# Reordered sums of squares and projection products in the attention heads of a two-layer encoder

## What is computed

```python
h = layer_norm(x, ln_in_g, ln_in_b)
for l in range(DEPTH):
    proj = h @ w_in[l]
    a_q, a_k, a_v, b_u, b_b, b_c, c_u, d_q, d_k, d_v = split_columns(proj)
    out_a = windowed_gqa_sink(...)      # group A: window of 128, sink, 4 query heads
    out_b = short_conv_mixer(...)
    out_c = fourier_mixer(c_u)
    out_d = dense_gqa_blocks(...)       # group D: dense attention, 4 query heads
    mix = jnp.concatenate([rms_norm(o, g[...]) for o in (out_a, out_b, out_c, out_d)], axis=-1)
    h = layer_norm(DN_ALPHA * h + mix @ w_out[l], ln1_g[l], ln1_b[l])
    ffn = jnp.square(jax.nn.relu(h @ w1[l])) @ w2[l]
    h = layer_norm(DN_ALPHA * h + ffn, ln2_g[l], ln2_b[l])
```

## Time and profile before

| | |
|---|---|
| time, median of 3 runs | 1057.16 us (1056.75 to 1057.83) |
| the profiled execution | 1057.18 us, span 1055.1 us |
| TensorE matmuls busy | 1038.5 us, 98% of the span |
| VectorE | 761.5 us, 72% |
| ScalarE | 532.4 us, 50% |
| GpSimd | 116.8 us, 11% |
| granted TensorE clock | 0.998 of full speed |

### The profile page before, as it was taken

One profiled execution on the slowest core, in us unless ns is written; L12 is line 12 of the kernel. 1 busy time (PEld: TensorE's weight loads), 2 busy tenths in 40 slices (PEclk: granted clock), 3 DMA queues, 4 the chain that ended last, 5 costly groups with the idle time before them and its releaser, 6 DMA issues.

```text
span 1055.1 us, 15201 instructions
## 1 busy us (share of the span) xinstructions
PE 1038.5 (98%) x5281; PEld 868.7 (82%) x5281; DVE 761.5 (72%) x1035; ACT 532.4 (50%) x777; POOL 116.8 (11%) x122
## 2 busy tenths in 40 slices
PE   7999999999999999999999999999999999999996
PEld 6888887988888888888888888879888888888885
DVE  7845876878668757758887558677884884785787
ACT  3433666665355255355634247666634643642654
POOL 5200343200000000000002004331000000000003
PEclk9999999999999999999999999999999999999999
DMA  8432023031521521521243410311243134125122
GB/s 292 160 120 80 1 61 121 9 121 59 187 74 40 199 80 40 174 106 53 108 144 139 160 41 22 120 42 49 80 157 122 40 124 156 40 92 186 40 80 80
DMA packets 17378, 105.47 MB, mean 100 GB/s; under 512 B 2016, under 2 KB 2704, under 8 KB 5792
## 3 DMA queue, kind: packets, MB, share of 16 engines
q1 hardware_dynamic: 15984, 98.70, 26.3%
q0 software_dynamic: 1184, 5.86, 1.7%
q10 hardware_dynamic: 144, 0.07, 0.0%
HBM read 101.49 MB, written 2.10 MB: 98 GB/s over the span
## 4 chain that ended last, share of the span: by engine, by line
PE 94%; POOL 2%; issue 1%; ACT 1%; DMA 1%; DVE 0%; DVEq 0%; SPq 0%; POOLq 0%; ACTq 0%
PE bank L465 19%; PE bank L466 18%; PE bank L467 18%; PE bank L815 9%; PE bank L814 9%; PE bank L813 9%; PE bank L753 2%; PE bank L738 2%; PE bank L474 1%; PE bank L644 1%; PE bank L645 1%; POOL w_lo L1816 1%; PE bank L541 1%; POOL x L1911 1%; PE bank L548 1%
## 5 line engine op out<-in xcount | busy, mean ns | idle before, releaser
L465 PE MATMUL bank<-h_hi,w_hi 128*128 128x512 f32 (+1 forms) x688 | 257.8, 375 | 0.0
L466 PE MATMUL bank<-h_lo,w_hi 128*128 128x512 f32 (+1 forms) x688 | 257.5, 374 | 0.0
L467 PE MATMUL bank<-h_hi,w_lo 128*128 128x512 f32 (+1 forms) x688 | 257.5, 374 | 0.0
L813 PE MATMUL bank<-w_hi,hid_hi 128*128 128x512 f32 x448 | 174.4, 389 | 0.0
L815 PE MATMUL bank<-w_hi,hid_lo 128*128 128x512 f32 x448 | 174.3, 389 | 0.0
L814 PE MATMUL bank<-w_lo,hid_hi 128*128 128x512 f32 x448 | 174.3, 389 | 0.0
L1257 DVE TENSOR_TENSOR w_lo<-w_raw,w_hi 128x2048 fp32r<-128x2048 f32 x62 | 141.8, 2287 | 39.2 <-ACT w_hi L929 32.7
L929 ACT CAST w_hi<-w_raw 128x2048 fp32r<-128x2048 f32 x56 | 107.1, 1913 | 85.8 <-PE bank L815 61.5
L466 PEld LDWEIGHTS bank<-h_lo,w_hi 128*128 128x128 f32 x688 | 129.5, 188 | 23.1
L465 PEld LDWEIGHTS bank<-h_hi,w_hi 128*128 128x128 f32 x688 | 129.5, 188 | 23.0
L467 PEld LDWEIGHTS bank<-h_hi,w_lo 128*128 128x128 f32 x688 | 129.5, 188 | 23.1
(11 more groups left out here) (184 smaller groups left out, 1610.3 us busy)
## 6 DMA issues: line engine op xcount, KB each, us to landing
w_raw<-in_weights SPq DMA_DIRECT2D x63, 1024.0 KB, 4.7
w_third<-in_weights SPq DMA_DIRECT2D x23, 1024.0 KB, 4.8
rows<-in_rows POOLq DMA_DIRECT2D x4, 1024.0 KB, 4.7
w_raw<-in_weights SPq DMA_DIRECT2D x4, 512.0 KB, 8.5
out_h<-x SPq DMA_DIRECT2D x8, 256.0 KB, 2.0
x<-in_x SPq DMA_DIRECT2D x3, 512.0 KB, 9.6
dft<-in_dft SPq DMA_DIRECT2D x2, 512.0 KB, 7.0
qk_gain<-in_qk_gain POOLq DMA_DIRECT2D x3, 192.0 KB, 3.5
```

The lines of the kernel that those rows point to most:

```text
L465: pe.matmul(dst, s_hi, m_hi, start=first, stop=False)
L466: pe.matmul(dst, s_hi, m_lo, start=False, stop=False)
L467: return pe.matmul(dst, s_lo, m_hi, start=False, stop=last)
L813: pe.matmul(bank[dst + t][:], s_hi, m_hi, start=start, stop=False, skip_group_check=goes_on)
```

## The change

On TensorE, in `SIDE_STEPS`, the second product of tile 3 of group 2 goes from step 11 to step 12, and the second product of tile 0 of group 3 from step 13 to step 14; DVE's additions (and the statistics and variance of tile 0) move with them. In every even step from 4 to 14 the sum of squares comes behind the transposes of the probabilities. Behind the loop TensorE takes the probabilities of the last pair, then the products of tile 2 (they need quad 6), the sum of quad 6, the values of pairs 14 and 15 in one run, the inverse of quad 7, the second half of tile 0, tile 1, and then the products of tile 3 with the sum of quad 7 between them. On ScalarE the high copy of the second half of tile 0 goes behind the squares of quad 7. On DVE the first low half of tile 0 and the two additions of tile 2 go ahead of the scaling of quad 7, the second low half and tile 1 behind its low part, and its mean behind those. GpSimd's and SP's programs are not changed.

```diff
-    SIDE_STEPS.update({4 * _g + _t: w_items(_g, _t, _t + 1) for _t in range(TOK)})
+    SIDE_STEPS.update({4 * _g + _t: w_items(_g, _t, _t + 1) for _t in range(TOK) if (_g, _t) != (2, 3)})
 SIDE_STEPS[3] = [("s", 1)] + SIDE_STEPS[3]
-SIDE_STEPS.update({13: w_items(3, 0, 1), 15: w_items(3, 1, 2), 16: w_items(3, 2, 4)})
+SIDE_STEPS.update({11: [("w", 2, 3, 0)], 12: [("w", 2, 3, 1)], 13: [("w", 3, 0, 0)], 14: [("w", 3, 0, 1)],
+                   15: w_items(3, 1, 2), 16: w_items(3, 2, 4)})
...
 # TensorE
                         turn_inverse(quad_scaled_in(p))
+                    for u in pair(p - 1):
+                        turn_probs(u)
                     if quad_high_in(p) is not None:
                         sum_quad(quad_high_in(p))
-                    for u in pair(p - 1):
-                        turn_probs(u)
                 wait(pe, l, "probs", UNITS)
                 turn_half(l, 1, 0, 0)
-                take_values(PAIRS - 2)
                 for u in pair(PAIRS - 1):
                     turn_probs(u)
-                sum_quad(6)
-
-                turn_half(l, 1, 0, 1)
-                take_values(PAIRS - 1)
-                turn_inverse(7)
                 last_sides = list(sides_of(PAIRS))
                 side(last_sides[0])
                 side(last_sides[1])
-                sum_quad(7)
+                sum_quad(6)
+                take_values(PAIRS - 2)
+                take_values(PAIRS - 1)
+                turn_inverse(7)
+                turn_half(l, 1, 0, 1)
                 turn_stream(1)
                 side(last_sides[2])
+                sum_quad(7)
                 side(last_sides[3])
...
 # ScalarE
                 copy_inverse(7)
-                stream_high_tile(0)
+                stream_high(l, 1, 0, 0)
...
                 wait(act, l, "head_out", 8)
                 mix_high_quad(7)
                 square_head_out(7)
+                stream_high(l, 1, 0, 1)
                 stream_high_tile(1)
...
 # VectorE
                 mix_low_quad(6)
                 normalise_first(l, 1)
                 mean_quad(6)
-                scale_quad(7)
-                stream_low(l, 1, 0)
+                low_half(l, 1, 0, 0)
                 last_sides = list(sides_of(PAIRS))
                 side(last_sides[0])
+                side(last_sides[1])
+                scale_quad(7)
                 mix_low_quad(7)
-                side(last_sides[1])
+                low_half(l, 1, 0, 1)
+                stream_low(l, 1, 1)
                 mean_quad(7)
-                stream_low(l, 1, 1)
                 side(last_sides[2])
                 side(last_sides[3])
```

## The result

The changed kernel takes 1073.23 us (median of 4 runs, 1070.71 to 1073.62) against 1057.12 us (1056.75 to 1057.83): a ratio of 1.0147, 95% interval 1.0129 to 1.0164. The profiled execution took 1072.88 us, 15.7 more than that of before. The forecast was 1066.5 with a range of 1061.5 to 1069.0: the direction was right, the size was not.

What follows compares the result with a forecast made beforehand. TensorE's instruction stream plus its waits was taken as the bound. Per layer -0.81 + 2.25 + 0.05 + 3.2 = +4.7 us, +9.4 in two layers, gave 1066.5 us, range 1061.5 to 1069.0.

Steps and rivals of the forecast that it cites:

- Step 12, -0.81: TensorE's wait at the sum of squares of quad 4, covered by moved product and transposes: -0.81 us per layer.
- The other sums at nothing: Sums of squares of steps 4, 6, 8, 10 moved behind transposes: no cost; up to 0.83 us each if uncovered.
- Step 14, a wait of 3.05: TensorE's wait at the sum of quad 5, behind GpSimd's root of tile 0: 3.05 us replacing 0.80, +2.25 per layer.
- The disturbance of GpSimd by DVE's centring: GpSimd's addition of quad 5's squares lengthened while DVE centres tile 0: 0.43 us taken, between 0 and 0.97.
- First wait of the end, 0.7: TensorE before the products of tile 2, waiting for quad 6's low part: 0.7 us, net about +0.05 per layer.
- Second wait of the end, 3.2: TensorE before the third product of the end, waiting for DVE's low part of quad 7: +3.2 us per layer.
- the clock falls: Rival: work behind four 3 us waits partly runs at 1.2 GHz, 1.5 us lost each; 1072.5 us, chance 0.04.
- The most that reordering can return: TensorE's existing waits at sums of quads 4, 5 and values of pairs 14, 15: 2.26 us per layer, some 4.5 altogether.
- The 0.2 for the weight load of pair 15: TensorE's real wait at the weight load of pair 15's values, taken as 0.2 us from between 0 and 0.35.

## Why the prediction was right and wrong

*Step 12, -0.81:* right. From the first scores of step 11 to those of step 13 it is 170.78 - 161.94 = 8.84 us, before 170.95 - 161.26 = 9.69: -0.85. But half of the reason was wrong: the sum behind the transposes alone wins nothing (1057.63), so it is the product that comes along that does.

*The other sums at nothing:* right, no wait is seen at them and the kernel with the sums alone does not move.

*Step 14, a wait of 3.05:* right in road and size, 2.69 + 0.16 = 2.85. The disturbance of GpSimd by DVE's centring was taken as 0.43; it is (0.70 - 0.55) + (0.66 - 0.45) = 0.36 over the root and the addition. The Trainium skill (SBUF — State Buffer, "SBUF: two separate sides") has the later instruction wait for the earlier to end. By that, as an estimate, the addition, which starts 0.38 into the centring (181.62 against 181.24), would have ended its plain 0.45 behind the first half of a pair of 1.58, at 182.03 + 0.45 = 182.48; it ended at 182.28. The row lies between no disturbance and the rule.

*First wait of the end, 0.7:* the number is right (0.50 + 0.16), and in part by luck: the road was only one of two. DVE's scaling behind tile 1 makes it 1.45 where TensorE is not held up in step 14; the new wait there is what let the 0.7 come out.

*Second wait of the end, 3.2:* right, 3.00 + 0.16. That the half and the two additions hold up quad 7 is shown by moving the half alone: the wait falls to 0.65, where 0.7 was named for that case.

*The clock:* here the prediction failed. The sum held TensorE's own work at its old length ("TensorE's own work stays as long as it is"); it grew by 7.2 us of busy time, and 7.3 us went when the waits were filled. The rival "the clock falls" was given a chance of 0.04, and a granted clock that leaves 1.00 was named as a sign of the forecast failing: it left it, to between 0.73 and 0.93 in the windows. That rival came true on top of the forecast, with its place, its number of falls and nearly its price: 1.5 for each wait, measured 1.6 to 1.8; its time was 1072.5, and 1073.2 came out. That it came so near has luck in it: the 1.5 was half of the wait's length, and a fall's price does not follow the wait (a 3.00 with no fall, a 2.69 with twice the price). The mistake was in the chance. No row of before showed a wait of 3 us within the heads, so that no row spoke against a fall; the only row on an idle TensorE spoke for it, at 0.64. A change that is forecast to add four waits of a kind not seen before should have had this rival near one half, or its price in the range. The section of the Trainium skill that stood beside it (TensorE: Matmul & The Clock Gate, "HAM oscillation — how this bites in real kernels") says that the work behind each idle gap starts at the lower clock again and pays every time; the windows of the changed kernel agree that each gap pays, 1.7 us, while in layer 0 the work starts at the full clock, and with the new end alone one gap of two paid nothing.

*The sum:* per layer, from the values of step 9 to the start of the hidden tiles, it is 207.52 - 155.09 = 52.43 us against 199.29 - 154.46 = 44.83, +7.6. With the waits filled it is 49.25, so 3.2 of this is the clock and 4.4 the waits, where 4.7 were forecast; the terms as measured, -0.85 + 2.05 + 0.0 + 3.16, make the same 4.4. Twice 7.6 and the 0.6 ahead of the heads of layer 0 make 15.8 of the 16.0 by which the span grew.

*"The most that reordering can return", 4.5 us:* as a bound it held, as a sum to be won it did not. A wait shown before an instruction is no sum to be won: the two of 0.65 were covered by the exponents' ring. The 0.2 for the weight load of pair 15 has no support either: the same 0.35 stands before the weight load at 174.82 of the kernel before, where no engine ended it. The best order that was run wins 3.4: 1.3 by filling the steps with products, the rest by taking out waits of step 15 and of the end.

## What to carry to other kernels

When a reordering is forecast to make TensorE wait longer than it does anywhere in the kernel now, price the work behind the wait at the lower clock as well: here four waits of some 3 us bring a loss of 8.8 us by themselves (1065.95 against 1057.12) and 7.3 by the clock, and needless matmuls in the wait give the second part back. Before an idle time is counted as to be won, look for what the next instruction on that engine would wait for if it came sooner. When work moves that ends a chain (the last addition of a tile), follow what it starts into the queues of the other engines, and put the instruction that someone waits for ahead of the one that only continues the chain.

## What the runs showed of the hardware

In the profiled executions the granted clock left 1.00 behind 11 of 12 idle times of 2.69 and 3.00 us, and behind none of those of 0.50 to 1.48; between them no run lies. The one without a fall is a 3.00, in layer 1 of the new end alone. What such a fall costs is not fixed: mostly 1.7 us of full clock, once 3.4 (behind a 2.69, in layer 1 of the kernel with the half later). In layer 0 of the changed kernel the matmuls became slow only 0.6 to 0.8 us after TensorE had begun again, so that the first rows behind a wait don't show it; in layer 1 the first rows do. The kernels with falls also spread more: the changed kernel's runs lie 2.9 us apart, those with the waits filled 0.6. With 4 runs each, this is seen and not proved; a number of falls that differs from run to run would explain it.
